# Attention values over merged value rows plus a masked triangle times a difference, chains of one count, and the output weights' maximum later in the last unit

## The reference

```python
def window_attention(q, k, v, k_buf, v_buf, pos0, sinks, rel_table):
    ...
    dist = WINDOW + j - c
    mask = (dist >= 0) & (dist < WINDOW) & (key_pos >= 0)
    ...
    p = jnp.exp(s - m[..., None])
    denom = jnp.sum(p, axis=-1) + jnp.exp(sink - m)
    o = jnp.einsum('bnhgqk,bnkhd->bnqhgd', p / denom[..., None], vb)
```

## Time and profile before

| | |
|---|---|
| median of 3 runs | 2035.23 us (2035.08 to 2035.64) |
| the profiled execution | 2040.07 us, span of its instructions 2038.2 us |
| PE busy | 1972.1 us, 97% |
| VectorE busy | 1666.0 us, 82% |
| ScalarE busy | 876.3 us, 43% |
| GpSimd busy | 303.6 us, 15% |
| mean granted clock of TensorE | 0.983 of 2.4 GHz |

### The profile page before, as it was taken

One profiled execution on the slowest core, in us unless ns is written; L12 is line 12 of the kernel. 1 busy time (PEld: TensorE's weight loads), 2 busy tenths in 40 slices (PEclk: granted clock), 3 DMA queues, 4 the chain that ended last, 5 costly groups with the idle time before them and its releaser, 6 DMA issues.

```text
span 2038.2 us, 36656 instructions
## 1 busy us (share of the span) xinstructions
PE 1972.1 (97%) x12974; PEld 1100.8 (54%) x12974; DVE 1666.0 (82%) x4034; ACT 876.3 (43%) x2246; POOL 303.6 (15%) x288
## 2 busy tenths in 40 slices
PE   5899999999999999999988999999999999999998
PEld 3555555555555555445455555555555555554453
DVE  7788888888888888664566888888888888898656
ACT  7744445444444446231264444444444444552100
POOL 2011111111111111020010111111111111111100
PEclk9999999999999999999999999999999999999989
DMA  9222222222222224885631222222222222457552
GB/s 333 43 45 57 60 49 49 49 58 60 49 49 49 57 60 130 203 261 135 205 113 57 50 50 49 69 49 49 49 49 62 54 59 50 92 149 199 139 133 96
DMA packets 303428, 184.17 MB, mean 90 GB/s; under 512 B 267847, under 2 KB 277000, under 8 KB 303180
## 3 DMA queue, kind: packets, MB, share of 16 engines
q1 hardware_dynamic: 287348, 151.41, 30.2%
q0 software_dynamic: 7424, 29.43, 4.0%
q10 hardware_dynamic: 8568, 2.18, 0.5%
HBM read 85.29 MB, written 41.06 MB: 62 GB/s over the span
## 4 chain that ended last, share of the span: by engine, by line
PE 85%; DVE 10%; ACT 2%; issue 2%; DMA 1%; DVEq 0%; ACTq 0%
PE J L589 52%; PE J L1328 14%; PE W L1027 2%; PE W L1016 2%; PE W L1101 2%; DVE W L580 1%; PE W L1131 1%; PE W L1119 1%; PE W L1090 1%; PE T L1110 1%; PE J L1065 1%; PE W L1034 1%; PE T L1075 1%; PE W L1103 1%; PE W L1134 1%
## 5 line engine op out<-in xcount | busy, mean ns | idle before, releaser
L589 PE MATMUL J<-W,x_mix 128*128 128x512 f16 (+2 forms) x3072 | 610.6, 356 | 2.8 <-issue 2.8
L589 PE MATMUL J<-W,uT_mix 128*128 128x512 f16 (+2 forms) x3072 | 609.6, 355 | 2.7 <-issue 2.4
L589 PEld LDWEIGHTS J<-W,x_mix 128*128 128x128 f16 x3072 | 298.3, 99 | 273.1 <-issue 11.5
L589 PEld LDWEIGHTS J<-W,uT_mix 128*128 128x128 f16 x3072 | 297.8, 99 | 272.4 <-issue 9.9
L1444 ACT ACTIVATE PB<-J,out_scale 128x512 f32<-128x512 f32 (+2 forms) x224 | 133.0, 594 | 288.0 <-PE J L589 279.9
L1328 PE MATMUL J<-W,EM_qkR_mix 128*128 128x512 f16 x480 | 115.3, 379 | 0.0
L2367 POOL TENSOR_TENSOR ST<-HH,ge 128x512 f32<-128x512 f32 x32 | 41.4, 1294 | 408.7 <-DVE HH L1853 408.7
L2376 POOL TENSOR_TENSOR ST<-ST,ge 128x512 f32<-128x512 f32 x32 | 67.8, 2119 | 216.7 <-DVE ST L1898 216.7
L1328 PE MATMUL J<-W,x_mix 128*128 128x512 f16 x400 | 99.6, 389 | 0.0
L1408 ACT ACTIVATE sc_xr<-sc_xr,small 128x128 f32<-128x128 f32 x256 | 98.6, 386 | 0.0
L1328 PE MATMUL J<-W,uT_mix 128*128 128x512 f16 x400 | 98.0, 384 | 0.0
(11 more groups left out here) (470 smaller groups left out, 3471.7 us busy)
## 6 DMA issues: line engine op xcount, KB each, us to landing
W<-in_w_in POOLq DMA_DIRECT2D x8, 2048.0 KB, 10.4
mix_d<-ST SPq DMA_DIRECT2D x32, 512.0 KB, 2.6
sc_xr<-in_x_prompt SPq DMA_DIRECT2D x20, 512.0 KB, 4.1
sc_xr<-x SPq DMA_DIRECT2D x20, 512.0 KB, 3.8
ST<-in_w_in POOLq DMA_DIRECT2D x4, 2048.0 KB, 11.4
W<-in_w_out SPq DMA_DIRECT2D x4, 2048.0 KB, 8.8
PB<-in_x_prompt SPq DMA_DIRECT2D x6, 512.0 KB, 3.7
x<-PB SPq DMA_DIRECT2D x6, 512.0 KB, 3.5
```

What stands on the lines that cost most here:

```text
L589: mm = nc.tensor.matmul(out, stationary(k, a), moving[:, k, b, :], start=(k == 0 and n == 0), stop=(k == KT - 1 and n == 2))
```

## The change

1. Values. The masked copies for the two blocks go. The transposed probabilities `pT` stay whole, with 64 keys of each half past or current for all queries of the other half. `v16[:, odd]` and `v16[:, 1-odd]` become merged rows: for queries 0 to 63, rows 0 to 63 are the current block's and the rest the past one's; for queries 64 to 127 all rows are the current block's. The merged product is right but for the triangle of keys j > i inside the same half. There the masked probabilities `pT_tri` (64 x 64 per head and half) times the difference past minus current, `dv16`, are added. The sums of the two query halves are in two banks, `B[0]` and `T[0]`.
2. Making the operands: VectorE's `v_diff` and `v_change_lo`, ScalarE's `v_change_hi`, and at a layer's start `v_same`, on the new counter `v_steps` (4 a chunk), which also takes the place of `k_lo`.
3. `part_probs` masks only the two 64-row halves. `values` waits on `em_masked`, `v_steps` and `pT_loaded`, and from its third pair of parts on `pT_ready`.
4. VectorE's chains all count 10 a unit: the last step raises the semaphore by the rest.
5. Last unit: `r_keys` and `top_of_all` move behind the attention's values on VectorE; `top_turn` moves behind `turn_back`, `top_spread` behind aq; `w_out_scale` and the high and low halves move behind aq's evacuation, `q_lo` and the new operands, two low halves ahead of `r_weights`.
6. Four small buffers are placed inside `small_p`; a constant mask is smaller.

```diff
             def step(self, ins):
                 self.k += 1
-                ins.then_inc(self.sem, 1)
-                self.eng.wait_ge(self.sem, self.base + self.k)
+                last = self.k == self.steps
+                ins.then_inc(self.sem, 1 + self.counts - self.steps if last else 1)
+                self.eng.wait_ge(self.sem, self.base + (self.counts if last else self.k))
...
+        oT_banks = [B[0], T[0]]
...
             def values(n, attn, odd):
-                pe.wait_ge(E["pT_ready"], n)
-                terms = [(s, a, b) for s in range(1 if attn == "first" else 0, 2) for a, b in ((0, 0), (0, 1), (1, 0))]
-                for i, (s, a, b) in enumerate(terms):
-                    v, p = v16[:, 1 - odd if s else odd], pT_cur if s else pT_past
-                    for kv in range(A_KV):
-                        mm = MM(B[0][half(kv), :], v[:, a, HD * kv:HD * kv + HD], p[:, b, 4 * kv:4 * kv + 4, :],
-                                start=(i == 0), stop=(i == len(terms) - 1))
+                pe.wait_ge(E["v_steps"], keep(pe, 4 * n))
+                pe.wait_ge(E["pT_loaded"], keep(pe, 16 * n))
+                terms = ((0, 0), (0, 1), (1, 0))
+                for i, (a, b) in enumerate(terms):
+                    if i == 2:
+                        pe.wait_ge(E["pT_ready"], n)
+                    for c in range(2):
+                        v = v16[:, 1 - odd if c else odd]
+                        for kv in range(A_KV):
+                            MM(oT_banks[c][half(kv), 0:256], v[:, a, HD * kv:HD * kv + HD],
+                               pT[:, b, 4 * kv:4 * kv + 4, half(c)], start=(i == 0), stop=False)
+                for i, (a, b) in enumerate(terms):
+                    for c in range(2):
+                        for kv in range(A_KV):
+                            mm = MM(oT_banks[c][half(kv), 0:256], dv16[half(c), a, HD * kv:HD * kv + HD],
+                                    pT_tri[half(c), b, 4 * kv:4 * kv + 4, :], start=False, stop=(i == 2))
                 mm.then_inc(E["oT_psum"], 1)
...
                 project_block(n, "akv", odd)
+                pe.wait_ge(E["em_masked"], n + 1)
                 values(n, attn, odd)
                 m_out(n)
-                if not more:
-                    top_turn(pe, layer, W_OUT)
                 pe.wait_ge(E["em_masked"], n + 1)
                 r_turn(n, T[1])
                 turn_back(n)
                 if not more:
+                    top_turn(pe, layer, W_OUT)
+                project_block(n, "aq", odd)
+                if not more:
                     top_spread(pe, layer, W_OUT)
-                project_block(n, "aq", odd)
...
             def values_back(n):
                 act.wait_ge(E["oT_psum"], n)
-                af(qTA_part[:], B[0], ACT.Copy, scale=v_scale[:, 1:2]).then_inc(E["oT_ready"], 1)
+                for c in range(2):
+                    op = af(oTA[:, :, 64 * c:64 * c + 64], oT_banks[c][:, 0:256].rearrange("p (t q) -> p t q", t=4),
+                            ACT.Copy, scale=v_scale[:, 1:2])
+                op.then_inc(E["oT_ready"], 1)
...
+            def v_change_hi(n, odd):
+                act.wait_ge(E["v_steps"], 4 * n + 3)
+                af(v16[0:64, 1 - odd, 0, :], PB[0:64, AV:AV + P], ACT.Copy, scale=v_scale[0:64, 0:1])
+                cp(v16[0:64, 1 - odd, 1, :], v16[0:64, odd, 1, :])
+                af(dv16[:, 0], v_change, ACT.Copy, scale=-1.0).then_inc(E["v_hi"], 1)
...
                     next_hi(n)
                     evac(n, "aq")
+                    v_change_hi(n, odd)
                     mix_hi(n)
                     gate_first(n, "r")
                 else:
                     gate_first(n, "r")
+                    evac(n, "aq")
+                    v_change_hi(n, odd)
                     act.wait_ge(E["m_out_psum"], n + 1)
-                    w_out_hi(act, layer, range(0, 3))
-                    evac(n, "aq")
-                    w_out_hi(act, layer, range(3, KT))
+                    w_out_hi(act, layer, range(0, KT))
...
-            def part_probs(n, attn):
+            def part_probs(n):
                 dve.wait_ge(E["pT_loaded"], 16 * n)
-                for s in range(1 if attn == "first" else 0, 2):
-                    kept = const("cur_t" if s else "past_t").bitcast(F16).unsqueeze(1).to_broadcast([P, 2 * A_HEADS, P])
-                    op = V.tensor_tensor(pT_both[s], pT_both[1], kept, ALU.mult)
+                for c in range(2):
+                    rows = half(c)
+                    past = const("past_t").bitcast(F16)[rows].unsqueeze(1).to_broadcast([64, 2 * A_HEADS, 64])
+                    op = V.tensor_tensor(pT_tri[rows].rearrange("p s h c -> p (s h) c"),
+                                         pT[rows, :, :, rows].rearrange("p s h c -> p (s h) c"), past, ALU.mult)
                 op.then_inc(E["pT_ready"], 1)
...
+            def v_same(n):
+                dve.wait_ge(E["v_hi"], 2 * n + 2)
+                V.scalar_tensor_tensor(v16[:, 1, 1, :], PB[:, AV:AV + P], v_scale[:, 0:1], v16[:, 1, 0, :],
+                                       ALU.mult, ALU.subtract).then_inc(E["v_steps"], 2)
+                V.memset(dv16[:].bitcast(F32), 0.0).then_inc(E["v_steps"], 1)
+
+            def v_diff(n, odd):
+                V.scalar_tensor_tensor(v_change, PB[:, AV:AV + P], v_scale[:, 0:1], v16[:, 1 - odd, 0, :],
+                                       ALU.mult, ALU.subtract).then_inc(E["v_steps"], 1)
+                dve.wait_ge(E["v_steps"], 4 * n + 2)
+                V.tensor_tensor(v_change, v_change, v16[:, 1 - odd, 1, :], ALU.subtract).then_inc(E["v_steps"], 1)
+
+            def v_change_lo(n, odd):
+                dve.wait_ge(E["v_hi"], 2 * n + 2)
+                V.scalar_tensor_tensor(dv16[:, 1], v_change, -1.0, dv16[:, 0], ALU.mult, ALU.subtract
+                                       ).then_inc(E["v_steps"], 1)
...
-                r_keys(n)
                 if more:
+                    r_keys(n)
                     norm_size(dve, n + 1, x_next)
                     norm_scale(dve, n + 1)
...
-                    top_of_all(dve, layer, W_OUT)
                 m_result(n)
                 values(n)
                 if more:
                     next_lo(dve, n + 1)
                 else:
-                    w_out_scale(dve, layer)
+                    top_of_all(dve, layer, W_OUT)
+                    r_keys(n)
                 dve.wait_ge(E["mixmr_ready"], n)
                 m_gated(n)
                 v_lo(n, odd)
+                v_diff(n, odd)
                 if more:
                     q_lo(n, NBLK * n + 7)
+                    v_change_lo(n, odd)
                     mix_size(n, keep(dve, c - 1))
                     r_weights(n)
                 gate_inverse(n, "r")
                 if not more:
-                    w_out_lo(dve, layer, range(0, 3))
                     q_lo(n, NBLK * n + 7)
-                    w_out_lo(dve, layer, range(3, 4))
+                    v_change_lo(n, odd)
+                    w_out_scale(dve, layer)
+                    w_out_lo(dve, layer, range(0, 2))
                     r_weights(n)
+                    w_out_lo(dve, layer, range(2, 4))
                     w_out_lo(dve, layer, range(4, KT))
```

More of the change, by code:

```diff
@@ L85 @@
                      ("mask_s", 64), ("dmat_s", 256), ("inter_s", 4), ("tail_s", 4), ("full_s", 2),
-                     ("own", 8), ("own4", 4), ("one", 1), ("slot3", 256), ("past", 128), ("cur_t", 64), ("past_t", 64)])
+                     ("own", 8), ("own4", 4), ("one", 1), ("slot3", 256), ("past", 128), ("past_t", 32)])
 C4, N4 = layout([("parity", 128), ("pair", 2), ("slot", 4), ("ones", 128), ("keep", 64), ("drop", 64),
@@ L135, in shape_constants @@
     put("past", i[None, :] > i[:, None])
-    now = i[:, None] <= i[None, :]
-    for name, on in (("cur_t", now), ("past_t", ~now)):
-        put(name, on.astype(np.float16).view(f))
+    put("past_t", (i[:, None] % 64 > i[None, 0:64]).astype(np.float16).view(f))
     put("own", np.arange(TS)[:, None] // DEC_SEQ == np.arange(DEC_BATCH)[None])
@@ L285, in build @@
         wmax = sb("wmax", [P, NBLK, KT])
[L286 to L287 removed]
+        gtop = small_p[:, 19:20]
+        wtop = small_p[:, 104:104 + NBLK]
         top_one = sb("top_one", [1, 1])
         wm = sb("wm", [P, 3])
[L290 removed]
+        gabs = small_p[:, 120:120 + KT]
         gs = sb("gs", [P, NBLK, KT])
@@ L335, in build @@
         sc = sc_xr2[:].rearrange("p (h c) -> p h c", h=A_HEADS)
-        pT_past, pT_cur = (ST[:, 1024 * i:1024 * i + 1024].bitcast(F16).rearrange("p (s h c) -> p s h c", s=2, h=A_HEADS)
-                           for i in range(2))
-        pT_both = [ST[:, 1024 * i:1024 * i + 1024].bitcast(F16).rearrange("p (g c) -> p g c", g=2 * A_HEADS) for i in range(2)]
+        pT_tri = ST[:, 0:512].bitcast(F16).rearrange("p (s h c) -> p s h c", s=2, h=A_HEADS)
+        pT = ST[:, 1024:2048].bitcast(F16).rearrange("p (s h c) -> p s h c", s=2, h=A_HEADS)
```

(8 more changed lines are left out.)

34 lines of the change are left out of this document (17 added, 17 removed).

## The result

The changed kernel took 2052.88 us in the median of five runs (2044.45 to 2053.32), the kernel before 2035.64 beside it (2035.08 to 2040.19): a ratio of 1.0065, 95% interval 1.0052 to 1.0078. By the ratio it is slower by some 13 us (17 between the medians), where 2026.8 was forecast. The profiled execution is the fastest of the five (2044.45). It had a mean granted clock of 0.987; the runs at 2053 had 0.982 to 0.984, and the kernel before 0.983 in its profile. So the two profiles, 4.4 us apart, show too little of the loss. Each run's time multiplied by its own granted clock, which takes most of that out, gives 2017.7 in the mean for the changed kernel, and 2005.0 for 23 runs of the kernel before in a later comparison: 12.7 more.

What follows compares the result with a forecast made beforehand. TensorE (PE), busy 97% of the span, was taken as the bound. Middle units -6.24, first units +0.84, output-stage `values` -0.48, last units -2.85, `r_out` waits +0.3: together -8.4, 2035.2 to 2026.8 us; range 2024.0 to 2033.5.

Steps and rivals of the forecast that it cites:

- PE's part: TensorE's `values` in each unit: 1.41 us becomes 1.17 with four quarters side by side, 0.24 less a unit.
- Rival D: In `values`, quarters overlap in pairs only: 1.50 us, +0.09 in 28 units, 2037.1 us in all; chance 0.04.
- The equal counts of the chains: VectorE's chain counts: they alter register work, which runs under the instructions; no cost given.
- VectorE's ring: VectorE's own time per middle unit, with ScalarE's short steps: 46.26 becomes 46.49 us, 0.12 under PE's 46.61.
- the masking: VectorE's `part_probs`: 2.35 us becomes two operations on 64 lanes taking 1.25, saving 1.10 a unit.
- The new operands: VectorE and ScalarE, from the second `v_lo` to `mix_size`: 0.92 us becomes 2.25, +1.33 a unit.
- the whole 0.59 ahead of `r_result`: VectorE's mean wait for PE in a middle unit, before L1831, taken off 46.85 to give 46.26 us.
- Rival B: VectorE's ring or `r_out`'s wait eats the middle units' gain: 2030.4 us at +0.26, 2033.1 at +0.36; chance 0.19.
- No wait at L537: Layer 0's last unit: PE no longer waits 2.3 us for the output weights' maximum; first output half 3.3 earlier.
- Rival C: VectorE's half masking operations go at half rate, 1.2 us each, deciding from 0.80: 2053.5 us in all; chance 0.08.
- Rival E: Waits before and in the first output half bring the lower clock; layer 0's 3.3 us are lost: 2030.1; chance 0.09.
- the 2.85: Gain from the two layers' last units together: 3.3 us won in layer 0, 0.45 lost in layer 1.

Runs made afterwards that it cites:

- a_oldcounts: The changed kernel with each VectorE chain counting its own steps again, nothing else: 2051.91 us, ratio 1.0066 to the kernel before.
- b_counts: The kernel before with the equal counts of 10 a unit for VectorE's chains alone: 2041.55 us, ratio 1.0014.
- e_lo_later: The changed kernel with v_change_lo placed behind r_weights instead of ahead of mix_size: 2037.5 us, ratio 0.9994 to the kernel before.
- d_order_only: The kernel before with only the later order for the output weights in a layer's last unit, on PE, ScalarE and VectorE: 2037.45 us, ratio 1.0001.
- j_old_order: e_lo_later with the order before for the output weights on all engines, PE waiting for values_back ahead of the turn: 2032.87 us, ratio 0.9977 to the kernel before.
- h_stores: e_lo_later with the nine writes of the prompt's states put behind the transposition of the last probabilities on SP's queue: 2048.58 us, ratio 1.0058 to the kernel before.

## Why the prediction was wrong, step by step

- PE's part held in kind: four quarters side by side, the change of shape inside paid. It gains 0.18 to 0.19 a unit, not 0.24; with nothing in its way PE's period is 46.66, 46.61 forecast. Rival D falls.
- "The equal counts of the chains alter register work, which runs under the instructions": this is the step that failed. A chain's last step that raises by more than one has an extra instruction there, five more a unit; together 0.37 us a unit in VectorE's ring (a_oldcounts, b_counts), against the 0.12 to spare. It was put at nothing without a row behind it.
- The ring's terms that had a price: the masking saved 0.86 from start to start, not 1.10; its operations of 64 lanes take 0.69 each and no longer overlap. The new operands cost 1.09, not 1.33. The two errors cancel: +0.23, as forecast.
- Taking the whole 0.59 ahead of `r_result` for spare was too much. The ring without that wait starts `r_result` at once, and then `mix_lo` runs beside GpSimd's product: 1.54 in the mean instead of 1.28 in the changed kernel, 1.50 in layer 0 with own counts. With this term the sums close: 46.26+0.23+0.22 = 46.71 with own counts, 46.71 measured; 46.26+0.23+0.37+0.26 = 47.12 in the changed kernel, 47.07 measured. The term is read from the traces; no run takes it out alone.
- Rival B was the mechanism, VectorE's ring above all and `r_out` with 0.09 of it, and it went past its own end: at +0.36 it was to give nothing, and here +0.37 for the counts and +0.26 for `mix_lo` made the period 47.07, +0.22 on 46.85 where -0.24 was forecast. That is 26 x 0.46 = 12 us of the 21 between forecast and measurement at equal clock. e_lo_later shows it directly: 0.47 taken out of the ring, and 12.2 us come back. The first units cost 1.14 and 0.88 more than before, not 0.42 each: 1.2.
- "No wait at L537 ... layer 0's last aq block at 5.3 and full clock" held. From the last `values` to the end of the first output half it was 24.15 after and 27.75 before (gain 3.6, 3.3 forecast), in layer 1 24.14 and 24.10. But that it came out so near is partly luck: the 27.75 is from one long execution, and the three other kernels with the old order took 25.5 to 25.7, a gain of 1.4 to 1.5. And a price that I gave no term stood behind it: the transposition that comes 3.6 us forward without what is issued ahead of it, and 3.3 us of PE's wait. The order alone is worth nothing (d_order_only).
- Rival C (operations at half rate) had nearly the right time, 2053.5, for a wrong reason: they took 0.69, under the 0.80 from which it would decide.
- Rival D's 2037.1 was mis-added: its own terms give 2036.7. Rival E's lower clock did not come in the changed kernel; it came at an output stage in j_old_order, with another order.
- With 12 us for the middle units, 1.2 for the first ones and 3.3 for the wait in the output stage some 4 of the 21 are left. About 2 of them may be the long last unit of the profile before, from which the 2.85 was worked out; the rest stays open.

## To carry to other kernels

Slack is to be measured on each crossing of two engines, and idle time at a wait is not all free: an engine that starts earlier there can meet another one's work that it used to miss, here for a quarter of a microsecond a unit. An operation that has to wait for another engine's short steps belongs where its engine stands idle anyway; here that place was two lines further down and worth 12 us. A single profile can be a long case: a price taken from one wait in it is safer with a second execution beside it. And an edit that looks like bookkeeping (counts, registers, a few instructions ahead of a loop) is to be priced like any other: by its instructions on the engine that has the least slack.

## What the runs showed of the hardware

- A loop's cost can hang on where its code begins. The same loop of 332 instructions on VectorE, moved by 40 instructions, loaded five packets of 8 KB in every pass and stood 2.6 to 2.8 us at the branch; a loop of 339 that loads in every pass stood 3.2 to 3.4. The changed kernel's equal counts save 32 instructions in the loop against own counts (307, 339) and so keep clear of it, at 0.37 us a unit.
- VectorE's operation of 1024 elements a lane that reads and writes beside a GpSimd operation takes longer by the time that they share, less some 0.2 us: 1.28 us alone or with under 0.2 shared, 1.47 with 0.39, 1.60 with 0.53.
- A step that waits and raises a semaphore by more than one costs some 0.07 us more than one that raises it by one (0.27 against 0.20 from start to start).
- Within one kernel the time follows the mean granted clock: e_lo_later took 2030.2 at 0.988 and 2042.8 at 0.981. A difference of 0.3% between kernels needs as many runs as these had, or the clock beside each.
- A transposition by DMA that took 5.4 us took 10.0 when the last small transfer ahead of it on the queue was issued 2 us before it instead of 4; with the states' writes behind it, it took 5.7 (h_stores).
- Behind a PE wait of 1.35 us at `r_out` the granted clock was 0.60 in the mean of 4 us in layer 1 of j_old_order; behind the same wait in layer 0 it was 1.00.
- The masking of 1024 f16 elements a lane on 64 lanes took 0.69 us, of 2048 on 128 lanes 1.18. Lanes and elements changed together, so no row says what either is worth.
